# Third inner job of the last feed-forward network: its low weights on GpSimd, its high weights earlier on ScalarE

## The reference, cut to what matters

```python
def swiglu(h, w_in, w_out):
    gate, up = jnp.split(h @ w_in, 2, axis=-1)
    return (jax.nn.silu(gate) * up) @ w_out

x = residual_post_norm(x, y, m[:, 5], 1.0, ln_gain[1], ln_bias[1])
x = residual_post_norm(x, swiglu(modulate(x, m, 2), ffn2_w_in, ffn2_w_out), m[:, 8], FFN_HALF, ln_gain[2], ln_bias[2])
```

## Time and profile before

| what | value |
|---|---|
| median of 3 runs | 1351.39 us (1348.08 to 1352.56) |
| profiled execution, its own time | 1350.71 us |
| its span in the profile | 1348.7 us |
| TensorE clock granted, mean | 0.994 of full speed |
| PE busy | 1325.4 us, 98% of the span |
| DVE busy | 799.3 us, 59% |
| ACT busy | 520.1 us, 39% |
| POOL busy | 74.2 us, 5% |

### The profile page before, as it was taken

How to read it: one execution, slowest core, us unless ns; L and a number is a source line. 1 busy time by engine, 2 the same in 40 slices (tenths; PEclk the granted TensorE clock), 3 DMA queues, 4 the chain that set the end, 5 groups by cost and what they waited for, 6 DMA issues and landing times.

```text
span 1348.7 us, 17711 instructions
## 1 busy us (share of the span) xinstructions
PE 1325.4 (98%) x7200; PEld 1117.2 (83%) x7200; DVE 799.3 (59%) x1138; ACT 520.1 (39%) x726; POOL 74.2 (5%) x83
## 2 busy tenths in 40 slices
PE   8999999999999999999999999999999999999997
PEld 5777888888889999888888788887798888888886
DVE  5546578666786777565126778787853333433356
ACT  5535122222212544566234655555652231222211
POOL 1000000000000000000101111110000000000000
PEclk8999999999999999999999999999999999999999
DMA  9964545665545666553022112123425333333221
GB/s 319 292 177 137 194 155 171 182 182 173 175 156 156 185 185 183 172 175 117 23 72 70 48 48 62 48 63 97 122 74 160 102 103 94 96 101 108 86 63 62
DMA packets 206399, 175.00 MB, mean 130 GB/s; under 512 B 6906, under 2 KB 175464, under 8 KB 206320
## 3 DMA queue, kind: packets, MB, share of 16 engines
q1 hardware_dynamic: 197816, 142.74, 36.4%
q0 software_dynamic: 7808, 29.46, 6.6%
q10 hardware_dynamic: 696, 1.68, 0.3%
HBM read 171.74 MB, written 2.11 MB: 129 GB/s over the span
## 4 chain that ended last, share of the span: by engine, by line
PE 87%; DVE 5%; ACT 4%; issue 2%; DMA 1%; ACTq 0%; SPq 0%; DVEq 0%
PE ps L1945 27%; PE ps L1947 27%; PE ps L1946 27%; DMA w_raw<-ffn_w_in 1%; PE ps L1984 1%; DVE w_lo L1288 1%; ACT w_hi L835 1%; PE ps L2395 1%; PE ps L2380 1%; PE ps L1997 1%; PE ps L2143 0%; ACT x_squares L848 0%; PE ps L2414 0%; ACT hfull L864 0%; PE ps L2166 0%
## 5 line engine op out<-in xcount | busy, mean ns | idle before, releaser
L1945 PE MATMUL ps<-h_hi,w_lo 128*128 128x512 f32 (+1 forms) x1120 | 392.1, 350 | 1.2 <-DVE h_lo L1569 0.9
L1946 PE MATMUL ps<-h_lo,w_hi 128*128 128x512 f32 (+1 forms) x1120 | 388.6, 347 | 0.0
L1947 PE MATMUL ps<-h_hi,w_hi 128*128 128x512 f32 (+1 forms) x1120 | 388.5, 347 | 0.0
L1288 DVE TENSOR_TENSOR w_lo<-w_raw,w_hi 128x2048 fp32r<-128x2048 f32 (+1 forms) x107 | 237.1, 2218 | 167.5 <-ACT w_hi L835 167.4
L835 ACT ACTIVATE w_hi<-w_raw 128x2048 fp32r<-128x2048 f32 (+1 forms) x107 | 198.3, 1854 | 349.6 <-PE ps L1947 319.5
L1945 PEld LDWEIGHTS ps<-h_hi,w_lo 128*128 128x128 f32 x1120 | 212.2, 189 | 31.8 <-issue 5.0
L1947 PEld LDWEIGHTS ps<-h_hi,w_hi 128*128 128x128 f32 x1120 | 212.2, 189 | 27.1
L1946 PEld LDWEIGHTS ps<-h_lo,w_hi 128*128 128x128 f32 x1120 | 212.2, 189 | 25.4
L1310 DVE SCALAR_TENSOR_TENSOR ada_row<-ada_block,c_cols,ada_row 128x256 f32<-128x256 f32 x224 | 108.6, 485 | 8.0
L1449 DVE TENSOR_TENSOR glu<-ps,glu 128x512 f32<-128x512 f32 (+1 forms) x66 | 39.4, 597 | 121.8 <-ACT glu L895 121.8
L1945 PE MATMUL ps<-h_hi,half_lo 128*128 128x512 f32 (+1 forms) x272 | 102.0, 375 | 0.7 <-ACT beside_lo L1119 0.4
(11 more groups left out here) (272 smaller groups left out, 1771.4 us busy)
## 6 DMA issues: line engine op xcount, KB each, us to landing
w_raw<-ffn_w_in SPq DMA_DIRECT2D x124, 512.0 KB, 5.3
w_raw<-ffn_w_out SPq DMA_DIRECT2D x60, 512.0 KB, 4.2
ada_block<-w_ada POOLq DMA_DIRECT2D x28, 1024.0 KB, 5.7
half_raw<-w_mix_in SPq DMA_DIRECT2D x48, 256.0 KB, 3.3
ada_block<-w_ada SPq DMA_DIRECT2D x6, 1024.0 KB, 9.5
w_raw<-ffn_w_in SPq DMA_DIRECT2D x32, 128.0 KB, 6.1
w_raw<-w_mix_in SPq DMA_DIRECT2D x8, 512.0 KB, 4.2
w_raw<-ffn_w_out SPq DMA_DIRECT2D x12, 256.0 KB, 4.2
```

The lines of the kernel that those rows point to most:

```text
L1288: nc.vector.tensor_tensor(lo, raw, hi.bitcast(F32), ALU.subtract).then_inc(s_lo[s], 1)
L1945: nc.tensor.matmul(dst, s_low, m_high, start=start, stop=False)
L1946: nc.tensor.matmul(dst, s_high, m_low, start=False, stop=False)
L1947: return nc.tensor.matmul(dst, s_high, m_high, start=False, stop=stop)
```

## The change

ACT makes the high part of job 2 one step earlier: behind `centred_std("post", "lat", 1, 3)` and ahead of the squares of tile 2's second norm (`centred_std("pre", "lat", 2, 2)`; tile 2 is the third tile). DVE no longer makes the low part of job 2. POOL does, as the last instruction of its program, with a wait for the high part; the subtraction, its operands and the semaphore that it raises are the same.

```diff
@@ POOL, at the end of its program
+            third = slot_of(L2_FIRST + 2)
+            raw, hi, lo = split_views(L2_FIRST + 2)
+            pool.wait_ge(s_hi[third], USES[L2_FIRST + 2] + 1)
+            nc.gpsimd.tensor_tensor(lo, raw, hi.bitcast(F32), ALU.subtract).then_inc(s_lo[third], 1)
@@ ACT
             centred_std("post", "lat", 1, 3)
+            split_hi(L2_FIRST + 2)
             centred_std("pre", "lat", 2, 2)
-            split_hi(L2_FIRST + 2)
             modulate(PRE["lat", 2, 2], 0, 4)
@@ DVE
             post_finish("lat", 1, 3)
-            split_lo(L2_FIRST + 2)
             normalize("lat", 2, 3)
```

## The result

The changed kernel takes 1357.19 us (median of 11 runs, 1353.02 to 1358.59) against 1351.39 before (11 runs, 1348.08 to 1355.21): ratio 1.004, 95% interval 1.0031 to 1.005. It is slower, by a little more than the bound of 0.3%. The profiled execution took 1353.02, at the low end of its runs, with a span of 1351.1: executions of one and the same kernel lie up to 7 us apart (1348.08 to 1355.21 for before), more than the change moves, so the place itself is read in a measure of its own, within one profile. I call it the **passage**: from the start of tile 2's `post_center` to the end of tile 3's low part.

The account below looks back on a forecast made before the run. PE was taken as the bound, busy 98% of the span, stopping 1.06 and 1.28 us for DVE's normalised tiles. Terms 0 + 0 + 0 + 4.2 on 1351.39 gave 1355.6 us; 8 in 10 range 1351.2 to 1359.4.

Parts of the forecast that it names:

- the favoured case: POOL's read holds tile 2's `post_finish` on DVE, +4.2 us (+3.7 to +4.7), clock full, 1355.6 us; chance 50%.
- the first rival: Same DVE delay, and TensorE's clock falls in PE's 5.2 us stop: 2.5 us more (1 to 5), 1358.1 us; chance 27%.
- the hold: POOL's subtraction reading SBUF keeps DVE's `post_finish` of tile 2 out until 984.61 instead of 980.43: +4.2 us.
- The zeros: ACT's earlier copy, the low part's removal from DVE and SP's issue of job 4's weights: 0 us each.
- The copy in ACT's gap: Job 2's 1.90 us high part fits ACT's wait from 978.14 to 981.95, 1.9 us left: cost nothing.
- the low part off DVE: Removing 2.28 us from DVE at 985.94 only lengthens its wait for ACT's root to 2.9 us: gain 0.
- SP's earlier issue: Job 4's weights, issued at 988.25, go out when POOL is done; PE doesn't need them for tens of us: 0.
- my two ends: POOL's subtraction on 2048 elements, estimated between 4.0 and 5.06 us from shorter POOL operations; 4.5 taken.
- two rows: DVE's column add at 5.64 and low part at 820.25, held 1.05 and 0.85 us until 0.14 before POOL's end.
- my first two cases: DVE held 4.2 us with the clock full, 50%, or with TensorE's clock falling, 27%.
- the sum's last: Sum's terms 0 + 0 + 0 + 4.2 on 1351.39, with nothing for a fallen clock: 1355.6 us.
- The rival without hold: POOL's and DVE's reads do not collide, `post_finish` lasts 1.3 us, everything under cover: 1351.4 us; chance 13%.

Follow-up runs that it names:

- trimmed: Unchanged kernel, no POOL work: job 2's high part earlier, tile 3's squares ahead of tile 2's modulation, tile 2's high part on DVE; 1350.95 us, ratio 0.9997.
- pool_half: Against the changed kernel: POOL makes only columns 0 to 1023 of the low part, DVE the rest behind tile 3's `post_finish`; 1353.5 us, ratio 1.0017.
- changed, again: The changed kernel run once more, with no further edit, beside runs of the unchanged kernel on one chip; 1356.9 us, ratio 1.0045.
- act_alone: Against the unchanged kernel: only the earlier high part of job 2 on ACT, low part left on DVE; 1351.27 us, ratio 1.0.
- pool_alone: Against the changed kernel: high part put back behind tile 2's second squares, so only the low part's move to POOL remains; 1352.32 us, ratio 1.0005.
- write_only: Against the changed kernel: POOL does three memsets of the low part's tile instead of the subtraction, DVE makes the low part in its old place; 1351.78 us, ratio 1.0004.
- pool_later: Against the changed kernel: POOL also waits for tile 2's `post_finish` before its subtraction; 1356.48 us, ratio 1.0035.
- pool_twice: Against the changed kernel: POOL makes the subtraction twice, the second waiting for the first; 1360.55 us, ratio 1.0064.
- pe_filled: Against the changed kernel: 24 matmuls of 256 columns with unused results added on PE ahead of tile 2's turn; 1354.61 us, ratio 1.0027.

## Why the prediction was right, and where it was not

Forecast 1355.6 us, measured 1357.19: inside the range of 8 in 10 (1351.2 to 1359.4), and outside the 1354.6 to 1356.6 that the favoured case gave itself. What happened is the first rival, the hold with a fallen clock, whose own figure was 1358.1. The table has every profile but that of `trimmed` (on the first stops see `pool_half`).

| kernel | hold | PE's stop | clock | passage | against 17.34 |
|---|---|---|---|---|---|
| before | 0 | 1.06 | full | 17.34 | |
| changed | 4.21 | 5.28 | 0.50 | 22.42 | +5.08 |
| changed, again | 4.25 | 5.02 | 0.50 | 22.46 | +5.12 |
| act_alone | 0 | 1.06 | full | 17.35 | +0.01 |
| pool_alone | 0.95, tile 3 | 1.06, then 2.23 | full | 18.19 | +0.85 |
| pool_half | 2.06 | 2.83 | full | 19.39 | +2.05 |
| write_only | 0 | 0.77 | full | 17.34 | 0 |
| pool_later | 4.20, `post_center` | 4.99 | 0.50 | 22.14 | +4.80 |
| pool_twice | 4.25 + 3.86 | 8.61 | 0.50 | 26.04 | +8.70 |
| pe_filled | 4.29 | 2.18 | full | 21.63 | +4.29 |

**The zeros held.** The copy in ACT's gap, the low part off DVE and SP's earlier issue were costed at nothing; `act_alone` shows the first, and DVE's wait of 3.71 us for ACT's root after the change shows that the freed time was none that anyone waited for. The list of PE's waits has none for POOL's low part and none for job 4's weights.

**The hold was right in place, row and size.** Forecast +4.2, measured 4.21; POOL 4.5, measured 4.55 where it waited for nobody, so the value between my two ends was well taken (the Trainium skill's 4497 ns for such an add, in GPSIMD Engine Reference, 3.1 Elementwise — side-by-side cycle accounting, agrees). That the 4.21 meets the 4.2 so closely is in part luck: POOL takes 0.05 more than the 4.5, and the hold ends 0.20 before POOL's row and not 0.14, and the two errors cancel. That POOL's reading excludes, and not POOL at work, was argued from two rows; `write_only` shows that POOL at work isn't enough, and `pool_half` that the hold goes with the length of the read.

**The choice between my first two cases failed.** The likeliest case kept the clock full, at 50%, and left a fallen clock to 27%. It fell in all four profiles in which PE stood 4.99 us or more and in none in which it stood 2.83 or less. "Against it: matmuls ran densely until the stop" was no argument at all. The price, though, was 0.9 us instead of my 2.5 for that rival. I had counted tile 2's turn (1.1, measured 1.97 - 1.09 = 0.88), and added the slow matmuls of job 1's second half, at twice their 2.9 us. They took 4.2, from the turn's end at 988.24 to 992.42: at 0.50 they began 0.21 us apart for 0.12, 1.8 times and not twice as long, and the last of them ran at full clock again. So they came to an end just as tile 3 was normalised: its turn begins at 992.39, `normalize` ends at 991.52 + 0.81, the same 0.06 us ahead as before. The half speed used up PE's own stop of 1.28 us and nothing more, as `pe_filled` shows, where the stop is back; in `pool_twice`, where the clock came back sooner, 0.72 of it is left. So the step that failed is the sum's last: 0 for the clock where 0.9 belongs, and 1355.6 + 0.9 = 1356.5 would have been nearer to 1357.19. That 1355.6 came as near as it did with the wrong case for the clock is luck: the case left out cost 0.9 us, and not the 2.5 or up to 5 that I gave it.

**What is left**, 5.8 between medians against 5.1 in the passage, is within the scatter (the interval of the ratio is 4.2 to 6.8 us); the second set of runs gave 5.3 (1356.9 against 1351.57).

The rival without hold would have needed `post_finish` to keep 1.3 us, and is out. POOL's row ends 0.19 to 0.20 us later than the hold does in all these runs (0.26 where `normalize` is held), for 0.14 in the earlier trace rows; why was not tried.

## What to carry to other kernels

An instruction moved to an idle engine isn't free because the engine is idle: look at what its inputs share. In these runs a GpSimd instruction that reads SBUF kept VectorE's instructions with two SBUF inputs out until 0.2 us before its own end, and one with a single input (`normalize`) too. So one long GpSimd instruction beside a chain of short VectorE steps costs that chain as much of its length as falls on it; such work belongs beside a stretch in which VectorE waits for others, and the later of two harmless-looking moves may be what puts it elsewhere. And where a stop of TensorE grows from one to five microseconds, add what a lower clock costs behind it (here 0.9 us), but only as far as the work at half speed outlasts what TensorE waits for next.

## What the runs showed of the hardware that I had not expected

- TensorE's clock was at 0.50 for the work behind stops of 4.99, 5.02, 5.28 and 8.61 us, although matmuls ran without a gap until then, and full behind stops of 0.55 to 2.83 us. It came back some 4.8, 5.2 and 5.4 us after PE had begun again behind the stops of 5.28, 5.02 and 4.99 us, and 3.1 us after the one of 8.61.
- At 0.50 a matmul of 256 columns began every 0.21 us for 0.12 at full clock: 1.8 times as long, not twice. The turn's eight transposes took 1.97 us for 1.09.
- A hold is not for two SBUF inputs alone: `normalize`, a tensor_scalar on 1024 float32 elements with one SBUF input, took 1.76 us instead of 0.81 behind POOL's read in `pool_alone`.
- The two engines take turns: a POOL instruction already waiting goes before VectorE's next, and a VectorE one already waiting before POOL's next (`pool_twice`, POOL 4.58 and then 5.37 us).
- A POOL memset of 2048 elements takes 2.04 us (three in 6.11) and cost `post_finish`, `post_center` and `normalize` beside it nothing (1.28, 1.28 and 0.81 us).
